# The feed-forward's normed input moved from 32 to 256 bytes past the weights' place within 512 bytes

## The reference

```python
xn = rms_norm(h, ffn_norm_g[layer])
h = h + conv_gated_mlp(xn, w_up[layer], conv_w[layer], conv_b[layer], w_down[layer])

def conv_gated_mlp(x, w_up, conv_w, conv_b, w_down):
    h = x @ w_up                      # [256, 1024] @ [1024, 5632]
    ...                               # causal depthwise convolution of width 3
    gate, val = jnp.split(acc, 2, axis=-1)
    return (jax.nn.gelu(gate) * val) @ w_down
```

## The kernel before

| operand | bytes past a multiple of 512 | read as |
|---|---|---|
| `whi`, `wlo` | 0 | stationary (feature-major) or moving (token-major) |
| `xth`, `xtl` | 0 | moving in `ssm_u`, `mq`, `gb`, `gm`, `ga`; otherwise stationary |
| `fth`, `ftl` | 32 | moving in all `up` projections |
| `memh`, `meml` | 0 | moving in `km`, stationary in `vm` |
| `hth`, `htl`, `oth`, `otl` | 0 | stationary |
| `kmT`, `vm` | 64 | plain float32 products |
| `cst` (with `ident`, the identity of the transposes) | 384 | moving in transposes |

## Time and profile before

### The profile page before, as it was taken

One profiled execution on the slowest core, in us unless ns is written; L12 is line 12 of the kernel. 1 busy time (PEld: TensorE's weight loads), 2 busy tenths in 40 slices (PEclk: granted clock), 3 DMA queues, 4 the chain that ended last, 5 costly groups with the idle time before them and its releaser, 6 DMA issues.

```text
span 991.0 us, 15869 instructions
## 1 busy us (share of the span) xinstructions
PE 966.5 (98%) x6191; PEld 849.8 (86%) x6191; DVE 696.4 (70%) x1072; ACT 547.1 (55%) x898; POOL 258.1 (26%) x196
## 2 busy tenths in 40 slices
PE   5999999999999999999999999999999999999997
PEld 4878889999978887899999988899877789888886
DVE  5999557778864688586777764558576755666785
ACT  6746646665744655755666554454454454555723
POOL 4891101667800021200445510003122300000030
PEclk9989999999999999999999999999999999999999
DMA  7622255665665552446656566565544445754452
GB/s 280 223 93 86 86 175 188 192 191 172 191 179 162 170 171 85 149 151 200 186 182 187 191 191 192 181 205 178 164 150 149 143 150 162 210 162 152 148 188 84
DMA packets 48474, 165.97 MB, mean 167 GB/s; under 512 B 6544, under 2 KB 7056, under 8 KB 48400
## 3 DMA queue, kind: packets, MB, share of 16 engines
q1 hardware_dynamic: 48400, 164.95, 53.3%
HBM read 162.83 MB, written 1.05 MB: 165 GB/s over the span
## 4 chain that ended last, share of the span: by engine, by line
PE 86%; DVE 9%; ACT 2%; issue 1%; DMA 1%; POOL 0%; SPq 0%; DVEq 0%; POOLq 0%; ACTq 0%
PE PJ L595 13%; PE PJ L597 13%; PE PJ L596 13%; PE PJ L590 10%; PE PJ L588 10%; PE PJ L589 10%; DVE wlo L1699 3%; PE PJ L551 2%; PE PJ L552 2%; PE PJ L553 2%; DMA raw<-weights_in 1%; PE T L1032 1%; PE PJ L712 1%; PE T L1023 1%; ACT whi L1091 1%
## 5 line engine op out<-in xcount | busy, mean ns | idle before, releaser
L1699 DVE TENSOR_TENSOR wlo<-raw,whi 128x1024 fp32r<-128x1024 f32 x294 | 371.2, 1293 | 97.7 <-ACT whi L1091 95.3
L1091 ACT ACTIVATE whi<-raw 128x1024 fp32r<-128x1024 f32 x294 | 303.3, 1062 | 78.5 <-DMA raw<-weights_in 68.7
L588 PE MATMUL PJ<-xthb,whi 128*128 128x256 f32 x864 | 243.0, 281 | 0.9 <-DVE wlo L1699 0.5
L590 PE MATMUL PJ<-xthb,wlo 128*128 128x256 f32 x864 | 242.3, 280 | 0.0
L589 PE MATMUL PJ<-xtlb,whi 128*128 128x256 f32 x864 | 241.4, 279 | 0.0
L595 PE MATMUL PJ<-whi,xthb 128*128 128x512 f32 (+1 forms) x432 | 176.0, 407 | 2.6 <-DVE wlo L1699 2.2
L596 PE MATMUL PJ<-wlo,xthb 128*128 128x512 f32 (+1 forms) x432 | 168.8, 391 | 0.0
L597 PE MATMUL PJ<-whi,xtlb 128*128 128x512 f32 (+1 forms) x432 | 168.7, 390 | 0.0
L588 PEld LDWEIGHTS PJ<-xthb,whi 128*128 128x128 f32 x864 | 163.0, 189 | 1.7 <-issue 1.5
L589 PEld LDWEIGHTS PJ<-xtlb,whi 128*128 128x128 f32 x864 | 163.0, 189 | 0.2
L590 PEld LDWEIGHTS PJ<-xthb,wlo 128*128 128x128 f32 x864 | 162.9, 189 | 0.0
(11 more groups left out here) (398 smaller groups left out, 1358.2 us busy)
## 6 DMA issues: line engine op xcount, KB each, us to landing
raw<-weights_in SPq DMA_DIRECT2D x294, 512.0 KB, 3.5
rt<-bmerge_in SPq DMA_DIRECT2D x6, 256.0 KB, 4.2
xres<-x_in SPq DMA_DIRECT2D x2, 512.0 KB, 5.9
memx<-mem_in SPq DMA_DIRECT2D x2, 512.0 KB, 4.0
y_out<-xn SPq DMA_DIRECT2D x4, 256.0 KB, 2.4
rowv<-rows_in SPq DMA_DIRECT2D x1, 576.0 KB, 11.1
ptmp<-bexp_in SPq DMA_DIRECT2D x2, 256.0 KB, 6.9
cex<-cexp_in SPq DMA_DIRECT2D x2, 256.0 KB, 9.0
```

Of the source, the lines that this page charges most:

```text
L588: pe.matmul(o, a, xh[:, k, :], start=(first and f % 2 == 0), stop=False, skip_group_check=True)
L590: m = pe.matmul(o, b, xh[:, k, :], start=False, stop=last, skip_group_check=True)
L1091: act.activation(whi[:, p % HIGHS, :], raw[:, p % LOADS, :], ACT.Copy).then_inc(hi_ready, 1)
L1699: dve.tensor_tensor(wlo[:, p % LOADS, :], raw[:, p % LOADS, :], whi[:, p % HIGHS, :].bitcast(F32), ALU.subtract).then_inc(lo_ready, 1)
```

## The change

The offset of `fth` in `xthb`, and of `ftl` in `xtlb`, goes from 8 floats (32 bytes) to 64 floats (256 bytes). `xtlb` needs 48 floats more for it (`xthb` has the room already), and the filler `lines` gives up 48. So everything behind `lines` keeps its place, and what lies between `xtlb` and `lines` moves up by 192 bytes: `kmT`, `vm`, the tables and the small tensors. No instruction is added, removed or reordered.

```diff
         xthb = sbt(ctx, "xthb", [P, KD * TOK + 128], F32R)
-        xtlb = sbt(ctx, "xtlb", [P, KD * TOK + 16], F32R)
+        xtlb = sbt(ctx, "xtlb", [P, KD * TOK + 64], F32R)
         (xth, xtl), (fth, ftl) = ([b[:, o:o + KD * TOK].rearrange("p (k n) -> p k n", k=KD) for b in (xthb, xtlb)]
-                                  for o in (0, 8))
+                                  for o in (0, 64))
...
-        sbt(ctx, "lines", [P, 120])
+        sbt(ctx, "lines", [P, 72])
```

## The result

The changed kernel takes 996.51 us (median of 4 runs, 996.08 to 997.15); the kernel before 990.95 us (4 runs). The ratio is 1.0054, with a 95% interval from 1.0041 to 1.0067: slower by 5.6 us. The forecast was +5.7 us, 997.1 us, worked out from a median of 991.44 us.

The account below looks back on a forecast made before the run. TensorE was taken to bound the kernel, busy throughout the up-projections. Terms of 3.5 us (layer 0) and 2.2 us (layer 1), with zero for what moves along, gave +5.7 us on 991.44, 997.1 us; range 974.5 to 1005.

Parts of the forecast that it names:

- What bounds the up-projections: Up-projections: they go as fast as TensorE goes, busy throughout both windows at clock 1.00, with 86% of the chain.
- The price at 256 is the price at 0: Up-projection products in both layers: at 256 bytes each takes 120.0 ns, as at 0, instead of 116.7 or 117.9.
- The sum's two terms: Up-projections, 1056 products a layer: 3.5 us more in layer 0 and 2.2 us more in layer 1, together +5.7 us.
- the meeting in mid-load: Up-projections: starting 256 bytes ahead, the moving read meets the weight load in its middle and pays the whole surcharge, 120.0 ns.
- two points of a curve: Up-projection pace against operand distance: the earlier trace shows only 0 and 32 bytes, so the price at 256 could differ.
- What moves along is free: Tensors moved up by 192 bytes, read by transposes and plain float32 products: effect taken as zero.
- The far end of 5.5 us: Some 500 transposes, whose identity moves from 384 to 64: at worst a loss of 11 ns each, 5.5 us.
- A: Up-projections: reads hinder each other by starting together, so 256 gives 115 to 109 ns, 974 to 986.5 us; chance 0.34.
- B: Up-projections: 32 and 256 are both out of step, 116 to 119 ns, -3 to +4 us about 991.4; chance 0.17.
- C: Up-projections: the moving read catches the load and follows it, 121 to 144 ns, 999 to 1047 us; chance 0.13.
- D: Up-projections: the skill's rule of independent read ports holds, so place has no effect, 991.4 us; chance 0.03.
- the forecast of 998.5 us: Whole kernel: the predicted sum added to the profiled execution of 992.79 us, instead of to the median.

Follow-up runs that it names:

- the second probe: Kernel before plus 48-product groups behind its end, per distance, after one, two or three transposes; at 16 bytes 113.2 ns behind one, 116.8 behind two.

## Why the prediction was right, step by step

**What bounds the up-projections.** Right. Every kernel here moved by what its up-projections' pace moved, to 1 us, but for the ones at 16, 112 and 368 bytes, where the stretch behind layer 0 grew by 4 to 5.7 us. (A slip in the reading of the earlier trace rows, without effect: the 69% of the chain are six lines, 588 to 590 and 595 to 597; with 551 to 553, nine lines, it is 75%.)

**The price at 256 is the price at 0.** Right, and to the nanosecond: 120.0 in both layers. The sum's two terms, 3.5 and 2.2 us, were measured as 3.1 and 2.3 us. The first is too large because 15 steps near 150 us stood for the whole of layer 0: its last three up-projections, behind the transposes, ran at 117.8 ns before and not at 116.7.

**The reason for it.** Half wrong. I gave two, and put first the one of the meeting in mid-load. The kernel at 288 bytes refutes it, since it has a meeting in mid-load too and runs at 991.02 us. The other one holds: within 256 bytes, 256 is 0. It was luck that the wrong reason named the same row as the right one. The step that the prediction called its weak point, two points of a curve, was indeed weak: between 0 and 32, at 16, a rhythm of 113.3 ns can hold. Why distance 0 costs most, and by what mechanism the distance sets the pace, no run shows.

**What moves along is free.** Right: 990.87 us with the shift alone, and 0.87 us for eight transposes in both kernels. The far end of 5.5 us that I kept for it was not needed.

**The rivals.** A (the farther apart the better) fails at its own distance, 120.0 ns. What it promised, 115 to 109 ns, exists elsewhere on the curve (113.3). Its lower end of 109 ns came from transposes; products of this type take 113 even at 128 moving columns, with the first step in it, and no group of 256 columns went below 113.2. B (32 and 256 both out of step) fails: 256 is locked at 120.0. But its remark that the pace out of step hangs on the start is what the second probe shows at 16 and 192, and what the kernel before shows at 32. C (the faster read gets stuck behind the load) fails: no distance has a pace of 121 ns. D fails, and with it, for these products, the rule of the Trainium skill that the next load takes nothing from the running matmul ("TensorE: Matmul & The Clock Gate", section "Part 2: What happens when you issue a matmul"): the same instructions take 984.0, 990.9 or 997.2 us by the distance alone.

**From the profiled execution to the median.** The profiled executions differ by 996.8 - 992.79 = 4.0 us only, the medians by 5.6. The execution of before had the lower clock level for longer early on: its mean granted clock up to 137 us is 0.96, against 0.99 after, and its first up-projection started 1.3 us later. Set against its own execution the forecast of 998.5 us was 1.7 too high; set against the median it was 0.6 too high.

## What to carry to other kernels

Where TensorE is busy throughout with loads and matmuls of nearly equal length, read the distance between the starts of neighbours, compare it for the same instruction in different stages, and if it differs, work out where the two operands lie: here the distance between them, counted within 256 bytes, moves a product between 113 and 120 ns, and the kernel by 13 us of 991. Measure the curve in a series of products behind the end of the kernel before moving anything, with more than one start for each place, try the best few places in the kernel, and measure 512-column products apart, for they like another place. A faster stage can shift what other engines do beside its end; look there when the counts in the window are better and the time is not.

## What the runs showed that I had not expected

- The steady paces are 113.3, 116.7 and 120.0 ns at many distances, which are 272, 280 and 288 periods at 2.4 GHz; others, as 117.8 and 118.7, lie between. What rule picks one is open; I know of no order in the curve beyond its repeat after 256 bytes.
- For the same distance two rhythms can hold, 3.5 to 4.4 ns apart in the second probe, chosen by one transpose ahead of them (16 and 192 bytes). In the kernels the rhythm changes in mid-layer, behind transposes. At 192 bytes, the best kernel here, the last three up-projections of layer 0 ran at the slower rhythm of 117.8 ns and the loss behind layer 0 stayed away, so its time hangs in part on how its rhythm happened to start, and another change ahead of the up-projections may move it. At 112 bytes all groups of the second probe agreed.
- Distance 0 is among the worst places for 256 moving columns (120.0 against 113.3 ns) and the best tried for 512 (233 against 239 ns with the first step in it).
- Behind a wait of 2.99 us of TensorE the granted clock was 0.50 from 274.00 to 279.80 us; with a wait of 0.94 us at the same place it stayed at 1.00.
